# GpSimd takes the low halves of eight weight blocks in the last group of a state-space layer

## The chip, the cores and the metric

The kernel runs on one core of a Trainium2 chip. The metric is the device time of one launch in microseconds (us), and lower is better. The engines of the core work side by side, each through its own instruction queue, and meet only at semaphores: TensorE (PE), VectorE (DVE), ScalarE (ACT), GpSimd (POOL) and SyncE (SP), which here only issues the weight transfers.

## The reference, cut to what matters

A two-layer transformer block (latent attention, a gated recurrence, two MLPs) is followed by a wide layer with three mixers and an MLP, all on 512 tokens, in float32. The third mixer is the state-space one (`ssd_mixer`), and the change lies in it:

```python
xbc = silu(causal_conv(xbc, conv_w, conv_b))
...
cb = einsum('bcign,bcjgn->bcijg', cm, bm)
y_diag = einsum('bcijg,bcijgh,bcjgh,bcjghp->bcighp', cb, lmat, dtc, xs)
...
y_off = einsum('bcign,bcghpn,bcigh->bcighp', cm, h_in, exp(a_cum))
y = y_diag + y_off + xs * d_skip
y = rms_norm_2(y * silu(z), norm_g)
...
gates = sigmoid(mg)
mix = gates[0] * (y_a @ w_br_dsa) + gates[1] * (y_b @ w_br_nsa) + gates[2] * (y_c @ w_br_ssd)
```

`lmat` and `exp(a_cum)` are decays, one 128x128 piece for each of four chunks of 128 tokens and each of 32 heads. The heads come in four groups of eight.

## The kernel before

**Weights.** All weight matrices lie in memory as blocks of 128 x 1024 floats (512 KB). SP streams them into a ring of four slots. A product in float32 is made of three passes of TensorE with rounded operands: high half of the weights by high half of the input (line 366), high by low (367), low by high (368). So each block is split first: `round_block` lets ACT write the high half, `ring_hi`, by one copy of 128x1024 (line 299), and `rest_block` subtracts it from the block and writes the low half, `ring_lo` (line 306). The halves lie in two slots in this stage, so the block n+2 can be rounded only when TensorE is done with block n. The semaphore `blocks_rounded` counts the high halves, and `blocks_split` the low ones, which must come in the order of the blocks whatever engine makes them.

**The state-space layer.** `ssd_pe`, `ssd_act`, `ssd_dve` and `ssd_pool` each write out one engine's part of four groups (`GRPS`) of ten steps (`STEPS`). Group g works on eight heads while the projections of group g+1 run on TensorE between its pieces. In the last group, g = 3, there is nothing left to project, and TensorE computes the eight blocks of the output gate (`ssd_gate`) in steps 0 to 7 in its place; the first two blocks of the next product, `ssd_out`, are split in steps 6 and 7. In a step s of the last group:

- PE: the cumulated decays of head s-1 (lines 2766, 2767); at even steps from 4 on the output of a pair of heads (`output`, lines 2779 and 2783), which waits for DVE's `decay` times `cb` of line 3002 of the step before; then gate block s (24 passes).
- ACT: two exponentials for head s-1, of which the first (line 2868) waits for DVE's differences (line 3012) and the second is line 2870; the copy of gate s out of PSUM (2874); `round_block` of gate block s+2 (299); then the squares of two tiles of y (2887) for the norm at the end, in `squares`. In step 1 the gate's copy and the rounding stand before the exponentials.
- DVE: `decay` times `cb` (3002), four differences (3012), at even steps from 4 on `pair_out` (3039, 3042), then `rest_block` of gate block s+2 (306), then `sums`, which adds ACT's two squares into `ssum` (3031; the first is a copy, 3029). In step 1 the states of the chunks (2979 to 2983) come first, then `rest_block`, then the differences. `sums` leaves out steps 0 and 8.
- POOL: three products in step 0 (3158), and in steps 1 to 8 one product of head s-1's decay with C (3163), `c_dec`, which waits for the first exponential and which PE's `output` needs.

After the last step DVE goes on to `ssd_out_dve` and PE to `ssd_out_pe`. POOL's queue then holds only two transfers, the reload of `h` late in `mix_out` and the store of the result.

```python
        dve.wait_ge(M.sem("blocks_rounded"), ...)
        dve.tensor_tensor(lo, M.ring[:, b % RING, :], hi.bitcast(F32), ALU.subtract).then_inc(M.sem("blocks_split"), 1)
```

Of the kernel before, what the change touches and what calls it, by code (L numbers as in the profile page):

```python
# [17 lines left out]
NT = D // P  # L18
# [15 lines left out]
GRPS, HPG = 4, 8  # L34
# [20 lines left out]
FIRST = {}  # L55
# [26 lines left out]
def splits_before(b):  # L82
    return sum(max(0, min(b, hi) - lo) for lo, hi in SPLITS)
# [199 lines left out]
def split_slot(M, b):  # L283

    if b < FIRST["dsa_in"] or b >= FIRST["ff_up0"]:
        return M.ring_hi[:, b % RING, :], M.ring_lo[:, b % RING, :], RING
    slot = splits_before(b) % 2
    return M.ring2_hi[:, slot, :], M.ring2_lo[:, slot, :], 2
# [13 lines left out]
def rest_block(dve, M, b, i=None, step=0):  # L302

    hi, lo, _ = split_slot(M, b)
    dve.wait_ge(M.sem("blocks_rounded"), (0 if i is None else i * step) + (splits_before(b) + 1))
    dve.tensor_tensor(lo, M.ring[:, b % RING, :], hi.bitcast(F32), ALU.subtract).then_inc(M.sem("blocks_split"), 1)  # L306
# [756 lines left out]
def split_dve(dve, src, hi, lo):  # L1063
    dve.tensor_copy(hi, src)
    dve.drain()
    dve.tensor_tensor(lo, src, hi.bitcast(F32), ALU.subtract)  # L1066
    return dve.drain()
# [1618 lines left out]
def c_dec_of(R, e):  # L2686
    return (R.c_dec + [R.acum, R.dt])[e % 4]
# [259 lines left out]
def ssd_dve(dve, M, R):  # L2947
# [27 lines left out]
    def states(g):  # L2975
        for c in range(N_STATE):
            dve.wait_ge(M.sem("ssd_added"), N_STATE * g + c + 1)
            if c == 0:
                dve.tensor_copy(R.state[1], M.bank(3))
            else:  # L2980
                dve.tensor_tensor(heads(R.state[c + 1]), heads(R.state[c]), by_head(R.chunk_decay, c, g), ALU.mult)
                dve.drain()
                dve.tensor_tensor(R.state[c + 1], R.state[c + 1], M.bank(3 + c), ALU.add)
            dve.drain().then_inc(M.sem("ssd_state"), 1)

    def mix(g, s):
        if s == 0:
            for c in range(QT):
                dve.wait_ge(M.sem("ssd_x_turned"), QT * g + c + 1)
                dve.tensor_tensor(heads(R.x_tok[c]), heads(M.bank(3 + c)), by_head(R.dtc, c, g), ALU.mult)\  # L2990
                   .then_inc(M.sem("ssd_xdt"), 1)
            dve.wait_ge(M.sem("ssd_cb"), g + 1)
            four = lambda x: x.rearrange("p (c i) -> p c i", c=QT)
            dve.tensor_tensor(four(R.cb), four(M.bank(7)), M.t("tri", P).unsqueeze(1).broadcast_to([P, QT, P]),
                              ALU.mult)
            dve.drain()
        if s >= 2:
            e = s - 2
            h = 8 * g + e
            dve.wait_ge(M.sem("ssd_decay"), h + 1)  # L3000
            decay = decay_of(R, g, e)
            dve.tensor_tensor(decay, decay, R.cb, ALU.mult).then_inc(M.sem("ssd_decay_cb"), 1)
        if 1 <= s <= 8:
            e = s - 1
            h = 8 * g + e
            dve.wait_ge(M.sem("ssd_cumulated"), h + 1)
            if h >= 4:
                dve.wait_ge(M.sem("ssd_out_mm"), 2 * (h // 2) - 2)
            for c in range(QT):
                w = slice(c * P, (c + 1) * P)  # L3010

                dve.tensor_scalar(decay_of(R, g, e)[:, w], M.bank(4 + e % 2)[:, w], R.acol[:, c, h:h + 1], 0.0,
                                  ALU.subtract, ALU.min)
            dve.drain().then_inc(M.sem("ssd_seg"), 1)  # L3014
        if s >= 4 and s % 2 == 0:
            pair_out(g, s // 2 - 2)

    def low(ks):
        for k in ks:
            dve.wait_ge(M.sem("tile_rounded"), k + 1 + split_before("ssd_norm"))  # L3020
            dve.scalar_tensor_tensor(out=R.y_lo(k), in0=R.y[:, k, :], scalar=M.c("ssd_norm", k),
                                     in1=R.y_hi(k).bitcast(F32), op0=ALU.mult, op1=ALU.subtract)\
               .then_inc(M.sem("norm_scaled"), 1)

    def sums(s):
        for k in ssd_squares(s):
            dve.wait_ge(M.sem("norm_squared"), k + 1 + M.past("ssd_norm", "squared"))
            if k == 0:
                dve.tensor_copy(M.ssum[:, :], M.sq[:, 0, :])
            else:  # L3030
                dve.tensor_tensor(M.ssum[:, :], M.ssum[:, :], M.sq[:, k % 2, :], ALU.add)
            dve.drain().then_inc(M.sem("norm_summed"), 1)

    def pair_out(g, k):
        pair = 4 * g + k
        dve.wait_ge(M.sem("ssd_gate"), pair + 1)
        dve.wait_ge(M.sem("ssd_out_mm"), 2 * (pair + 1))
        y = R.y[:, pair, :]
        dve.scalar_tensor_tensor(out=y, in0=R.conv[g % 2][k], scalar=M.c("ssd_d", pair),
                                 in1=M.bank(6 if pair % 2 == 0 else 3), op0=ALU.mult, op1=ALU.add)  # L3040
        dve.drain()
        dve.tensor_tensor(y, y, R.gate[g % 2][k], ALU.mult)
        dve.drain().then_inc(M.sem("ssd_y"), 1)
# [48 lines left out]
    for g in range(GRPS):  # L3092
        for s in range(STEPS):
            if s == 1:
                states(g)
            else:
                mix(g, s)
            if s == 9:
                if g + 1 == GRPS:
                    low(range(0, 4))  # L3100
                pair_out(g, 3)
            if g + 1 < GRPS:
                project(g + 1, s)
            elif s < NT:
                rest_block(dve, M, FIRST["ssd_gate"] + s + 2)
            if s == 1:
                mix(g, s)
            if g + 1 == GRPS:
                sums(s)
    ssd_out_dve(dve, M, R, low)  # L3110


def ssd_out_dve(dve, M, R, low):
    dve.drain().then_inc(M.sem("ssd_out_free"), 2)
    rest = lambda b: rest_block(dve, M, FIRST["ssd_out"] + b)
    low(range(4, 12))
    dve.wait_ge(M.sem("norm_root"), 1 + M.past("ssd_norm", "root"))
    dve.reciprocal(M.inv[:, 0:QT], M.root[:, 0:QT]).then_inc(M.sem("norm_inverse"), 1)
    low(range(12, 16))

    def scale(t):
        dve.wait_ge(M.sem("gates_ready"), NT + t + 1)
        dve.tensor_tensor(R.out_gate[t], R.out_gate[t], M.norm_bank("ssd_norm"), ALU.mult)
        dve.drain()

    rest(2)
    dve.wait_ge(M.sem("norm_spread"), 1 + M.past("ssd_norm", "spread"))
    scale(0)
    scale(1)
    for t in range(NT):  # L3130
        if t:
            rest(2 * t + 2)
        dve.wait_ge(M.sem("blocks_used"), FIRST["ssd_out"] + 2 * t + 2)
        m = M.m[:, t, :]
        dve.tensor_tensor(M.ssum[:, :], M.bank(2 * (t % 2) + 1), R.out_gate[t], ALU.mult)
        dve.drain()
        dve.tensor_tensor(m, m, M.ssum[:, :], ALU.add)
        dve.drain().then_inc(M.sem("ssd_out_free"), 1)
        rest(2 * t + 3)
        split_dve(dve, m, M.in_hi[:, t, :], M.in_lo[:, t, :]).then_inc(M.sem("mix_split"), 1)  # L3140
        if t + 2 < NT:
            scale(t + 2)


def ssd_pool(pool, M, R):
    heads = lambda x: x.rearrange("p (h d) -> p h d", d=64)

    def mix(g, s):
        if s == 0:
            if g:  # L3150

                pool.wait_ge(M.sem("ssd_out_mm"), HPG * g)
            for c in range(N_STATE):
                pool.wait_ge(M.sem("ssd_xdt"), QT * g + c + 1)
                if g == 0 and c == 0:
                    pool.wait_ge(M.sem("ssd_to_end"), 1)
                w = R.to_end[:, c, 8 * g:8 * g + 8].unsqueeze(2).broadcast_to([P, 8, 64])
                pool.tensor_tensor(heads(R.xw[c]), heads(R.x_tok[c]), w, ALU.mult).then_inc(M.sem("ssd_xw"), 1)
        if 1 <= s <= 8:
            e = s - 1  # L3160
            pool.wait_ge(M.sem("ssd_exp_c"), 8 * g + e + 1)
            c_dec = c_dec_of(R, e)
            pool.tensor_tensor(c_dec, c_dec, R.conv[g % 2][5], ALU.mult)\
                .then_inc(M.sem("ssd_c_dec"), 1)

    for g in range(GRPS):
        for s in range(STEPS):
            mix(g, s)

# [302 lines left out]
```

## Time and profile before

| | |
|---|---|
| runs | 2938.68, 2944.05, 2943.17 us; median 2943.17 us |
| the profiled execution | 2943.89 us; its span 2942.1 us |
| busy in the span | PE 94%, weight loads 75%, DVE 55%, ACT 39%, POOL 4% |
| the chain that ended last | PE 79%, DVE 11%, ACT 4%, issue 3%, DVE's queue 2% |
| mean granted clock of TensorE | 0.962 |
| steps 1 to 9 of the last group | about 2372 to 2427 us after the span's start |

The span runs from the first to the last instruction; the time of the execution is 1.79 us more. A share of busy time says how much of the span an engine had work in flight. The chain is followed back from the last instruction, at each step to what released it. "Issue" in it is time in which the engine waited for nothing that the profile shows.

### The profile page before, as it was taken

To read this page: it belongs to the slowest core of one execution; us is meant where nothing else is said; L and a number is where in the kernel's file an instruction comes from. 1 tells how busy PE (TensorE), PEld (TensorE's weight loads), DVE (VectorE), ACT (ScalarE), POOL (GpSimd) and SP (SyncE) were. 2 spreads that over 40 slices of the span, in tenths; PEclk is the share of its full clock that TensorE was granted. 3 is DMA by queue.
4 is the path that set the end of the run, shared out by engine and by line. 5 is a ranking of instruction groups with operands and counts; after the bars stand their busy time and mean duration, and the time that the engine had idled before them with its cause. 6 is when DMAs were issued, how large, how long until landed. Compare 5 with 4: busy or idle time off the path is not lost.

```text
span 2942.1 us, 38305 instructions
## 1 busy us (share of the span) xinstructions
PE 2752.9 (94%) x13735; PEld 2213.3 (75%) x13735; DVE 1610.6 (55%) x2960; ACT 1133.8 (39%) x1858; POOL 115.8 (4%) x102
## 2 busy tenths in 40 slices
PE   7999999989999899998998998999899989999998
PEld 5567888877888788887675885667677767778887
DVE  5335726445555672644756347754677765464452
ACT  4344322225554432222437325852255543232221
POOL 0000000000000000000130001000011110000000
PEclk9999999979999999997999989999899999999999
DMA  3112332312111233231120210012222222333231
GB/s 138 42 58 72 107 100 93 100 43 72 57 57 43 72 111 96 93 100 65 57 80 1 87 65 22 1 51 86 72 72 72 65 65 72 115 100 100 93 100 64
DMA packets 59647, 217.76 MB, mean 74 GB/s; under 512 B 6400, under 2 KB 6528, under 8 KB 59392
## 3 DMA queue, kind: packets, MB, share of 16 engines
q1 hardware_dynamic: 57920, 209.76, 22.7%
q0 software_dynamic: 1600, 6.29, 0.6%
q8 instruction: 81, 1.33, 0.2%
q14 instruction: 46, 0.38, 0.0%
HBM read 211.83 MB, written 4.19 MB: 73 GB/s over the span
## 4 chain that ended last, share of the span: by engine, by line
PE 79%; DVE 11%; ACT 4%; issue 3%; DVEq 2%; ACTq 0%; DMA 0%; POOL 0%; SPq 0%
PE ps L366 22%; PE ps L368 22%; PE ps L367 22%; PE ps L447 1%; DVE work L1862 1%; PE ps L500 1%; DVE big L2961 1%; DVE ring_lo L306 1%; DVEq L3014 1%; PE ps L751 1%; PE ps L1331 1%; DVE work L1881 1%; PE ps L455 1%; PE ps L1788 1%; ACT ring_hi L299 1%
## 5 line engine op out<-in xcount | busy, mean ns | idle before, releaser
L366 PE MATMUL ps<-a_hi,ring_hi 128*128 128x512 f32 x1936 | 779.7, 403 | 51.5 <-DVE ring_lo L306 25.4
L368 PE MATMUL ps<-a_hi,ring_lo 128*128 128x512 f32 x1936 | 765.8, 396 | 0.0
L367 PE MATMUL ps<-a_lo,ring_hi 128*128 128x512 f32 x1872 | 739.9, 395 | 0.0
L306 DVE TENSOR_TENSOR ring_lo<-ring,ring_hi 128x1024 fp32r<-128x1024 f32 x360 | 440.3, 1225 | 531.0 <-ACT ring_hi L299 501.7
L299 ACT ACTIVATE ring_hi<-ring 128x1024 fp32r<-128x1024 f32 x378 | 397.6, 1055 | 514.3 <-PE ps L368 512.1
L366 PEld LDWEIGHTS ps<-a_hi,ring_hi 128*128 128x128 f32 x1936 | 371.4, 192 | 134.7 <-issue 21.4
L368 PEld LDWEIGHTS ps<-a_hi,ring_lo 128*128 128x128 f32 x1936 | 370.8, 192 | 80.3
L367 PEld LDWEIGHTS ps<-a_lo,ring_hi 128*128 128x128 f32 x1872 | 359.0, 192 | 74.1 <-issue 1.2
L367 PE MATMUL ps<-hid_lo,ring_hi 128*128 128x512 f32 x960 | 375.5, 391 | 0.0
L366 PE MATMUL ps<-hid_hi,ring_hi 128*128 128x512 f32 x896 | 348.8, 389 | 1.5 <-DVE ring_lo L306 1.5
L368 PE MATMUL ps<-hid_hi,ring_lo 128*128 128x512 f32 x896 | 348.6, 389 | 0.0
L367 PEld LDWEIGHTS ps<-hid_lo,ring_hi 128*128 128x128 f32 x960 | 181.6, 189 | 37.7
L366 PEld LDWEIGHTS ps<-hid_hi,ring_hi 128*128 128x128 f32 x896 | 168.2, 188 | 36.7 <-DVE ring_lo L306 1.9
L368 PEld LDWEIGHTS ps<-hid_hi,ring_lo 128*128 128x128 f32 x896 | 168.2, 188 | 34.8
L1119 ACT ACTIVATE sq<-ps 128x512 f32<-128x512 f32 x96 | 57.5, 599 | 352.7 <-PE ps L368 304.9
L1137 DVE TENSOR_TENSOR ssum<-sq,ps 128x512 f32<-128x512 f32 x96 | 65.8, 685 | 87.8 <-ACT sq L1119 81.6
L1816 ACT ACTIVATE work<-work 128x128 f32<-128x128 f32 (+3 forms) x128 | 70.0, 551 | 11.1 <-DVE work L1866 11.1
L1752 PE MATMUL ps<-big,work 64*128 64x256 f32 (+3 forms) x384 | 64.6, 480 | 10.2 <-DVE work L1866 8.7
L1066 DVE TENSOR_TENSOR hid_lo<-ssum,hid_hi 128x512 f32 (+1 forms) x96 | 66.4, 692 | 12.7 <-issue 1.5
L1139 DVE TENSOR_TENSOR ssum<-ssum 128x512 f32<-128x512 f32 x96 | 66.5, 692 | 7.2
L1752 PEld LDWEIGHTS ps<-big,work 64*128 64x128 f32 x384 | 46.4, 204 | 28.4 <-issue 16.6
L1862 DVE CUSTOM_DVE_ANT_0 work<-ps,work 128x128 f32<-128x128 f32 (+3 forms) x128 | 54.9, 485 | 21.5 <-issue 21.5
(399 smaller groups left out, 3291.2 us busy)
## 6 DMA issues: line engine op xcount, KB each, us to landing
ring<-weights SPq DMA_DIRECT2D x392, 512.0 KB, 3.5
h<-x SPq DMA_DIRECT2D x1, 2048.0 KB, 9.1
residual<-h POOLq DMA_DIRECT2D x2, 1024.0 KB, 4.8
h<-residual POOLq DMA_DIRECT2D x1, 2048.0 KB, 10.9
out<-h POOLq DMA_DIRECT2D x1, 2048.0 KB, 7.8
tab<-tables SPq DMA_DIRECT2D x1, 1648.0 KB, 15.3
big<-positions SPq DMA_DIRECT2D x1, 256.0 KB, 3.5
col<-columns SPq DMA_DIRECT2D x1, 164.5 KB, 4.0
```

Of the source, the lines that this page charges most:

```text
L299: act.activation(hi, M.ring[:, b % RING, :], ACT.Copy).then_inc(M.sem("blocks_rounded"), 1)
L306: dve.tensor_tensor(lo, M.ring[:, b % RING, :], hi.bitcast(F32), ALU.subtract).then_inc(M.sem("blocks_split"), 1)
L366: pe.matmul(out, w_hi, hi, start=start, stop=False)
L367: pe.matmul(out, w_hi, lo, start=False, stop=False)
L368: return pe.matmul(out, w_lo, hi, start=False, stop=stop)
L1066: dve.tensor_tensor(lo, src, hi.bitcast(F32), ALU.subtract)
L1119: act.activation(M.sq[:, u % 2, :], M.bank(u % 4), ACT.Relu).then_inc(free, 1)
L1137: dve.tensor_tensor(M.ssum[:, :], M.sq[:, u % 2, :], M.norm_bank(norm), ALU.mult)
L1139: dve.tensor_tensor(M.ssum[:, :], M.ssum[:, :], M.ssum[:, :], ALU.mult)
L1752: mm = pe.matmul(M.ps[:, at:at + S_LEN[t]], self.staged[rows, u, t * P:(t + 1) * P], self.kinds[kind][0][rows, 0:S_LEN[t]], start=True, st ...
L1816: e = act.activation(s, s, ACT.Exp, bias=V.ntop[:, x, t:t + 1], scale=1.0, accum_out=V.sum[:, x, t:t + 1])
L1862: dve.tensor_tensor_reduce(V.p[x][:, CAUSAL_AT[t]:CAUSAL_AT[t] + S_LEN[t]], M.ps[:, at:at + S_LEN[t]], m[:, CAUSAL_AT[t]:CAUSAL_AT[t] + S_ ...
```

## The change

In the last group, the low halves of gate blocks 2 to 7 and of `ssd_out` blocks 0 and 1 are no longer written by DVE in its steps 0 to 7, but by GpSimd, behind its product of the same step. GpSimd waits once for all earlier low halves, and DVE waits once, ahead of the low half of `ssd_out` block 2, for GpSimd's eight.

```diff
@@ ssd_dve
             if g + 1 < GRPS:
                 project(g + 1, s)
-            elif s < NT:
-                rest_block(dve, M, FIRST["ssd_gate"] + s + 2)
             if s == 1:
                 mix(g, s)
@@ ssd_out_dve
+    dve.wait_ge(M.sem("blocks_split"), splits_before(FIRST["ssd_out"] + 2))
     rest(2)
@@ ssd_pool
     for g in range(GRPS):
         for s in range(STEPS):
             mix(g, s)
+            if g + 1 == GRPS and s < NT:
+                if s == 0:
+                    pool.wait_ge(M.sem("blocks_split"), splits_before(FIRST["ssd_gate"] + 2))
+                rest_block(pool, M, FIRST["ssd_gate"] + s + 2)
```

On DVE, steps 1 and 2 of the last group; `ps` is PSUM, `sq` the squares of ACT:

```order
 L2983 TENSOR_TENSOR work<-work,ps 128x512
-L306 TENSOR_TENSOR ring_lo<-ring,ring_hi 128x1024
 L3012 TENSOR_SCALAR work<-ps,work 128x128 x4
 L3029 COPY ssum<-sq 128x512
```

In step 1 the differences now stand right behind the states, and the copy of the first square behind them.

On DVE, steps 2 to 4, which the later steps repeat:

```order
 L3002 TENSOR_TENSOR work<-work 128x512
 L3012 TENSOR_SCALAR work<-ps,work 128x128 x4
-L306 TENSOR_TENSOR ring_lo<-ring,ring_hi 128x1024
 L3031 TENSOR_TENSOR ssum<-ssum,sq 128x512 x2
 L3002 TENSOR_TENSOR work<-work 128x512
 L3012 TENSOR_SCALAR big<-ps,work 128x128 x4
-L306 TENSOR_TENSOR ring_lo<-ring,ring_hi 128x1024
 L3031 TENSOR_TENSOR ssum<-ssum,sq 128x512 x2
 L3002 TENSOR_TENSOR big<-big,work 128x512
```

The two sums now stand right behind the differences; what they add, `sq`, is written by ACT behind the high half of the block.

On POOL, the last group:

```order
 L3158 TENSOR_TENSOR work<-work 128x512 x3
-L3163 TENSOR_TENSOR work<-work,big 128x512 x8
...
+L306 TENSOR_TENSOR ring_lo<-ring,ring_hi 128x1024
+L3163 TENSOR_TENSOR work<-work,big 128x512
+L306 TENSOR_TENSOR ring_lo<-ring,ring_hi 128x1024
+L3163 TENSOR_TENSOR work<-work,big 128x512
+L306 TENSOR_TENSOR ring_lo<-ring,ring_hi 128x1024
```

The eight products, one behind the other before, now have a low half ahead of each; the first belongs to step 0, and from step 1 on each product is followed by its step's low half.

## Rows read from the trace of the kernel before

**Rows 1.** Busy us by stretch: PE, PEld, DVE, ACT, POOL; then PEclk, DMA share, GB/s.

```profile
2386.50:2401.20 14.70, 13.86 (x82) 11.23 (x82) 10.84 (x19) 7.18 (x12) 2.58 (x2) 1.00 0.23 74
2427.00:2440.00 13.00, 9.51 (x44) 7.80 (x45) 10.81 (x16) 7.55 (x12) 0.00 (x0) 0.52 0.00 1
```

**Rows 2.** The chain that ended last, in step 3: start us, us, what.

```profile
2389.14 0.95 ACT ring_hi L299
...
2390.12 1.22 DVE ring_lo L306
2391.35 0.60 DVEq L3032
```

**Rows 3.** DVE in the last group, in time: start us, us, instruction [idle before].

```profile
2374.25 1.12 DVE L3012 TENSOR_SCALAR work<-ps,work 128x128 f32<-128x128 f32 x4
...
2377.10 0.58 DVE L3029 COPY ssum<-sq 128x512 f32<-128x512 f32 x1 [1.73 <-ACT sq L2887]
...
2378.62 0.69 DVE L3002 TENSOR_TENSOR work<-work 128x512 f32<-128x512 f32 x1
...
2385.75 0.69 DVE L3002 TENSOR_TENSOR work<-work 128x512 f32<-128x512 f32 x1
2386.36 1.12 DVE L3012 TENSOR_SCALAR big<-ps,work 128x128 f32<-128x128 f32 x4
...
2391.26 1.50 DVE L3031 TENSOR_TENSOR ssum<-ssum,sq 128x512 f32<-128x512 f32 x2
2392.88 0.69 DVE L3002 TENSOR_TENSOR big<-big,work 128x512 f32<-128x512 f32 x1
...
2395.62 1.56 DVE L3042 TENSOR_TENSOR big<-big,work 128x512 f32<-128x512 f32 x1
...
2421.86 0.69 DVE L3002 TENSOR_TENSOR big<-big,work 128x512 f32<-128x512 f32 x1
```

**Rows 4.** ACT in steps 1 and 3 of the last group.

```profile
2373.09 1.28 ACT L2868 ACT_TABLE_LOAD   x1
2375.43 0.60 ACT L2868 ACTIVATE work<-ps 128x512 f32<-128x512 f32 x1 [1.06 <-DVEq L3014]
...
2387.54 0.60 ACT L2868 ACTIVATE work<-ps 128x512 f32<-128x512 f32 x1 [3.55 <-DVEq L3014]
...
2389.03 1.06 ACT L299 ACTIVATE ring_hi<-ring 128x1024 fp32r<-128x1024 f32 x1
2389.98 1.15 ACT L2887 ACTIVATE sq<-big 128x512 f32<-128x512 f32 x2
```

**Rows 5.** POOL in time: a low half of an earlier stage, the products of steps 1 and 4.

```profile
1770.73 2.35 POOL L306 TENSOR_TENSOR ring_lo<-ring,ring_hi 128x1024 fp32r<-128x1024 f32 x1 [5.23 <-ACT ring_hi L299]
...
2376.11 1.30 POOL L3163 TENSOR_TENSOR work<-work,big 128x512 f32<-128x512 f32 x1 [16.42 <-ACT work L2868]
...
2395.35 1.29 POOL L3163 TENSOR_TENSOR work<-work,big 128x512 f32<-128x512 f32 x1 [5.84 <-ACT work L2868]
```

**Rows 6.** All low halves of POOL: busy us, mean ns | idle before, releaser.

```profile
L306 POOL TENSOR_TENSOR ring_lo<-ring,ring_hi 128x1024 fp32r<-128x1024 f32 x18 | 43.4, 2412 | 163.3 <-ACT ring_hi L299 163.3
```

**Rows 7.** DVE in time, beside the low half of Rows 5.

```profile
1771.79 1.44 DVE L2543 TENSOR_TENSOR work<-work 128x128 f32<-128x128 f32 x1
```

**Rows 8.** The four instructions of that line: ns min/median/max, first and last start.

```profile
L2543 DVE TENSOR_TENSOR work<-work x4: 293/294/1441, 1762.4 to 1778.1; 128x128 f32<-128x128 f32 x4
```

**Rows 9.** PE in time: decays of step 1, gate block 3, outputs of pairs.

```profile
2371.33 0.40 PE L2766 MATMUL ps<-ssd_sums,ssd_rows 128*128 128x512 f32 x1
...
2378.18 0.39 PE L366 MATMUL ps<-a_hi,ring_hi 128*128 128x512 f32 x1
...
2386.50 0.66 PE L2779 MATMUL ps<-work 128*64 128x128 f32 x8 [2.22 <-DVE work L3002]
...
2401.16 0.66 PE L2779 MATMUL ps<-big,work 128*64 128x128 f32 x8 [0.84 <-DVE big L3002]
...
2427.01 1.12 PE L2779 MATMUL ps<-big,work 128*64 128x128 f32 x8 [9.78 <-DVE big L3002]
```

## The prediction

> **What bounds the kernel now.** The table of the profile says where not to look first: PE is busy 94% of the span and DVE 55%. But the change touches 55 us in which this does not hold, so I read that stage by itself. The busy times by stretch show PE at 13.86 us of 14.70 there, at full granted clock: nearly full, not full [rows 1]. The chain of waits shows who sets the pace: in each step of the last group it goes through DVE's differences, ACT's exponentials, the gate's copy, ACT's high half, DVE's low half and DVE's sums, and back to the differences [rows 2]. PE is not on it; it is the one that waits for DVE's L3002, 2.22 us, 0.84 us and, at the end, 9.78 us [rows 9]. So what is worth anything here is the length of one turn of that chain.
>
> One turn, counted from L3002 of step 3 at 2385.75 (step 4's stands at 2392.88, so a turn is 7.13 us) [rows 3]: the differences end at +1.73 (2386.36 + 1.12); ACT's first exponential starts at +1.79, its high half runs from +3.28 to +4.34, and its two squares start at +4.23 and take 1.15 us, so the first is there at about +4.8 and the second at +5.38 [rows 4]. DVE's low half starts at +4.37 and takes 1.22 us; the first sum ends 0.60 behind it, at +6.20 [rows 2]; the second follows 0.12 later and takes 0.69, and 0.12 later is +7.13. The reader is to see that DVE's low half and ACT's squares run side by side: taking the former away leaves the latter.
>
> **The change part by part.**
>
> *Removed from DVE:* eight low halves. Of 1.22 us each only 0.65 could be won in steps 2 to 7: without them the first sum could start at about +4.86, behind the first square, end at +5.55, the second run to +6.36, and L3002 start at +6.48.
>
> *Added to POOL:* the same eight, at 2.41 us each, the mean of 18 [rows 6]. POOL follows ACT by 0.08 us (exponential 2375.43 + 0.60, product 2376.11) [rows 4, 5], so its low half runs from +4.42 to +6.83. POOL has the time: its product starts at about +2.5 and takes 1.29 us.
>
> *What the two do to each other* decides. In the stage of 1770 us a low half of POOL runs from 1770.73 to 1773.08 [rows 5]. DVE's L2543, which adds two small SBUF tiles, starts at 1771.79 in it and ends at 1773.23: 1.44 us where its median is 0.294 us [rows 7, 8]. It did not go slower in proportion, it ended when POOL had ended. The same in the last group: L3042 starts at 2395.62, beside POOL's product of 2395.35 to 2396.64, and ends at 2397.18 [rows 3, 5], 0.54 us behind POOL's end, about its own 0.69 us less the start. And L3029, a copy between SBUF tiles, takes 0.58 us and ends 0.27 us behind POOL's product, which ends at 2377.41 [rows 3, 5]. So DVE's work whose data all comes from SBUF waits for all of POOL's instruction. The sums of L3031 read two SBUF tiles, but no row of before has one beside POOL: that they wait too is the step I take without a row of their own. I take it because L3042 has the same form and size.
>
> The Trainium skill has this as a rule, in "SBUF — State Buffer", section "SBUF: two separate sides": DVE with two SBUF inputs and a GpSimd instruction that reads SBUF need the same pair of ports, and whichever comes first keeps it for its whole instruction. By that rule the sums wait, and the time is the forecast below; were it not to hold for them, it is the first rival.
>
> *One turn after,* steps 2 to 7: POOL's low half starts at +4.42, ahead of the first sum at +4.86. The sum ends 0.54 behind POOL's end, at +7.37; 0.12 + 0.69 + 0.12 later, at +8.30, is L3002. Six turns are 49.8 us. Before they were 2421.86 - 2378.62 = 43.24 us (two of them hold `pair_out`, which after lies in the same shade of POOL). So +6.56 us.
>
> *Step 1* has another order. DVE's differences no longer wait for the low half: PE's decays are there at about 2372 [rows 9], not 2374.25. ACT can use this only from the end of its table load, 2374.37; the exponential then comes 1.04 us earlier than 2375.43 [rows 4], the first square too, and the copy L3029 is asked for at 2376.06. But POOL's product now runs from 2375.07 to 2376.37, and its low half, 1.29 us behind the exponential instead of ahead of it, stands right behind. The copy ends at 2376.64, POOL holds DVE until 2379.05, the sum L3031 ends at 2379.59, and L3002 of step 2 starts at 2379.71 instead of 2378.62: +1.09 us. Other orders of the three give 2379.7 to 2380.0; I take the first. PE wants gate block 3 at 2378.18 [rows 9] and gets its low half at 2378.8 to 2379.9. This up to 1.7 us is hidden: behind it PE already waited 2.22 us for L3002 of step 3, which now starts 2.25 us later.
>
> *At no cost:* step 0, where POOL's low half (from about 2365) is wanted by PE only at 2372; the waits added on POOL and on DVE, whose counts are reached long before (POOL's eighth low half ends in step 7, two steps ahead of DVE's wait); step 8 and what follows, which have no low half, so all of the shift is passed on. What is queued behind POOL's low halves is its next product, asked for 4 us later. PE needs 2401.16 - 0.84 - 2386.50 = 13.82 us for a pair of heads with two gate blocks [rows 9]; DVE's two turns are then 16.6 us, so PE waits 2.8 us in each pair. If a low half were late for PE it would cost what it is late; the tightest, block 5, is ready at +6.83 of step 3, and PE, which starts its pair's output at +0.75, ends block 4 at about +8 (the output and one block are over half of 13.82).
>
> *Sum:* 6.56 + 1.09 = 7.65 us. The profiled execution's 2943.89 us would become 2951.5. It stands 0.72 us above the median of the runs, so I forecast 2943.17 + 7.65 = 2950.8 us, +0.26%. With a low half of 2.35 us and a stall that costs the sum 0.1 us less it is 6.6 us; if instead the first sum slips in ahead of POOL, POOL runs from +5.55 to +7.96, the second sum ends at +8.50 and the turn is 8.62 us, 9.6 us in all. So 2949.8 to 2952.8 if the mechanism holds.
>
> **The rivals.**
>
> *The sums do not wait (not slower).* Then the turn is 6.48 us, six are 38.9, which is 4.4 less than 43.24, and step 1 gives 1.04: -5.4 us, 2937.8 us. PE gives part of it back, since its 13.82 us for a pair are more than 12.96; I bound this case at -3.5 to -5.4 us, 2937.8 to 2939.7. For it: no row shows a sum beside POOL. Against it: L2543, L3042 and L3029. The point from which it decides: the sums end no later than before only if POOL holds them for less than about 1.2 us of its 2.41.
>
> *PE's granted clock falls.* PE would be busy 13.82 of 16.6 us, with gaps of 2.8 us. Behind the idle 9.78 us the granted clock is 0.52, the lower of its two levels [rows 1]; beside the gaps of 2.22 and 0.84 us it stays at 1.00. If it fell once in the middle, a gate block of 24 passes at 0.23 us would take up to some 5 us more, and the gaps absorb 2.8: 2 to 7 us on top, 2953 to 2958 us.
>
> *The extra is hidden.* The last group's end would have to be set by something else. PE's 9.78 us wait for L3002 of step 9 speaks against it, and so does the chain, which has no other member there. If half the turn's extra went unseen, the time would be about 2947.
>
> **How the numbers follow.** Forecast 0.80, the sums free 0.09, the clock 0.06, hidden in part 0.05. A measurement of this kernel can tell 0.2%, 5.9 us, from no change. The forecast's own range lies above it, by 0.7 us at the low end, so I leave 0.03 of it in "same". Slower: 0.77 + 0.06 = 0.83. Free sums straddle 0.2% from the other side, with most of their range within it: faster 0.04, same 0.05. So same is 0.03 + 0.05 + 0.05 = 0.13. The range reaches from halfway into the hidden case, with the scatter of the runs (5.4 us) in mind, to the middle of the clock's: 2945.5 to 2956. What lies in its lower part would be scatter; that part holds none of the free sums.
>
> **What would show it.** Right: on DVE the first L3031 of a step takes about 2.5 us in place of 0.69; eight POOL L306 of 2.4 us in the last group, each 0.08 us behind ACT's; L3002 every 8.3 us; PE's waits for L3002 near 2.8 us, and the last near 11. Wrong: L3031 at 0.69 us beside a running POOL L306 (first rival); passes of 0.43 us in a gate block (second); L3002 of step 2 at 2377.6 instead of 2379.7 (my reading of step 1); or a POOL L306 that itself is stretched by DVE, for which I have no price of its own in this stage.

## The result, and the profile after

| | before | changed |
|---|---|---|
| median of 16 runs | 2941.13 us (2936.57 to 2946.00) | 2948.55 us (2945.51 to 2953.40) |
| ratio | | 1.0026, 95% interval 1.0019 to 1.0033 |
| profiled execution, its span | 2943.89, 2942.1 us | 2945.70, 2943.9 us |

The changed kernel is 7.4 us slower by the medians, 0.25%. The forecast was +7.65 us and 2950.8 us. All 16 runs of before have a median 2 us below that of the three runs that the forecast started from, so the absolute time is 2.3 us lower than forecast and the difference 0.2 us. One of all the runs used here was slow, 3051.86 us at a granted clock of 0.878 (of the kernel "half a low half" below), and it is in no ratio.

The two profiled spans differ by 1.8 us only, since the profiled execution of before was 2.8 us above its median and that of the changed kernel 2.9 us below. So the spans can't be compared as a whole. A mark in DVE's program ahead of anything that the change touches shows why: L2994, the last product of step 0, starts at 2351.34 us, where it started at 2358.21 in the profile of before. The execution was 6.87 us ahead when it came to the stage, in code that is the same in both, which is within the scatter of the runs. I therefore measure the stage inside each profile, from the start of that L2994 to the start of DVE's first low half behind the group (of `ssd_out` block 2): 2449.28 - 2358.21 = 91.07 us before, 2449.80 - 2351.34 = 98.46 us after. That is +7.39 us, the whole of the loss. Each stage here is measured in one profile. Its last 23 us vary by up to 0.6 us from kernel to kernel with TensorE's clock (last section), so smaller differences are read at L3002, where that plays no part.

DVE in the changed kernel, in time (start us, us, instruction, idle before), which answers to [rows 3]:

```profile
2351.34 0.68 DVE L2994 TENSOR_TENSOR work<-ps,tab 128x512 f32<-128x512 f32 x1
...
2358.34 2.90 DVE L2981 TENSOR_TENSOR work<-work 128x512 f32<-128x512 f32 x1 [0.17 <-PE ps L2753]
...
2369.19 0.58 DVE L3029 COPY ssum<-sq 128x512 f32<-128x512 f32 x1 [2.93 <-ACT sq L2887]
2369.89 2.68 DVE L3031 TENSOR_TENSOR ssum<-ssum,sq 128x512 f32<-128x512 f32 x1
2372.69 0.69 DVE L3002 TENSOR_TENSOR work<-work 128x512 f32<-128x512 f32 x1
...
2377.59 3.26 DVE L3031 TENSOR_TENSOR ssum<-ssum,sq 128x512 f32<-128x512 f32 x2 [3.17 <-ACT sq L2887]
2380.96 0.69 DVE L3002 TENSOR_TENSOR work<-work 128x512 f32<-128x512 f32 x1
...
2385.86 3.30 DVE L3031 TENSOR_TENSOR ssum<-ssum,sq 128x512 f32<-128x512 f32 x2 [3.16 <-ACT sq L2887]
2389.27 0.69 DVE L3002 TENSOR_TENSOR big<-big,work 128x512 f32<-128x512 f32 x1
...
2397.94 0.69 DVE L3002 TENSOR_TENSOR big<-big,work 128x512 f32<-128x512 f32 x1 [0.47 <-issue]
...
2422.78 0.69 DVE L3002 TENSOR_TENSOR big<-big,work 128x512 f32<-128x512 f32 x1
...
2427.18 0.69 DVE L3002 TENSOR_TENSOR big<-big,work 128x512 f32<-128x512 f32 x1
...
2449.80 1.23 DVE L306 TENSOR_TENSOR ring_lo<-ring,ring_hi 128x1024 fp32r<-128x1024 f32 x1 [4.14 <-ACT ring_hi L299]
```

The two sums of a step took 1.50 us and take 3.3. DVE has one instruction less in each turn, is idle longer ahead of the sums (3.17 us for ACT's square where it was 2.65 for the high half), and yet a turn, from L3002 to L3002, is 8.27 and 8.31 us in steps 2 and 3, where it was 7.13.

POOL and the chain of waits of the changed kernel show what the sums wait for:

```profile
2349.77 3.05 POOL L3158 TENSOR_TENSOR work<-work 128x512 f32<-128x512 f32 x3 [12.35 <-DVE work L2990]
2358.31 2.39 POOL L306 TENSOR_TENSOR ring_lo<-ring,ring_hi 128x1024 fp32r<-128x1024 f32 x1 [5.49 <-ACT ring_hi L299]
...
2368.20 1.29 POOL L3163 TENSOR_TENSOR work<-work,big 128x512 f32<-128x512 f32 x1 [7.50 <-ACT work L2868]
2369.44 2.58 POOL L306 TENSOR_TENSOR ring_lo<-ring,ring_hi 128x1024 fp32r<-128x1024 f32 x1
...
2383.43 1.27 POOL L3163 TENSOR_TENSOR work<-work,big 128x512 f32<-128x512 f32 x1 [3.95 <-ACT work L2868]
2385.39 2.40 POOL L306 TENSOR_TENSOR ring_lo<-ring,ring_hi 128x1024 fp32r<-128x1024 f32 x1 [0.69 <-ACT ring_hi L299]
```

```profile
2384.36 0.95 ACT ring_hi L299
2385.31 0.53 ACT sq L2887
2385.83 0.02 issue
2385.86 2.48 DVE ssum L3031
2388.34 0.03 DVEq L3032
2388.37 0.09 issue
2388.46 0.69 DVE ssum L3031
```

The first sum is asked for at 2385.86, when POOL's low half has run for 0.47 us. POOL ends at 2387.79, and the sum at 2388.34, 0.55 us later; it took 2.48 us. The second sum, which meets nothing, takes 0.69. In the chain, the sum stands where the low half of DVE stood in [rows 2]. No semaphore joins the sum and POOL's low half, so here two engines meet outside the semaphores, and the profile shows it as a longer instruction, not as idle time.

The same happens once in step 1, which the prediction did not foresee: L2981, which reads two SBUF tiles, is asked for at 2358.34, when the low half of step 0 has just begun, and takes 2.90 us in place of 0.69, to 0.54 us behind POOL's end. It costs nothing, for the differences behind it wait for PE anyway, until 2365.13.

PE in the changed kernel, which answers to [rows 9]:

```profile
2372.16 0.47 PE L366 MATMUL ps<-a_hi,ring_hi 128*128 128x512 f32 x1 [0.69 <-POOL ring_lo L306]
...
2381.71 1.12 PE L2779 MATMUL ps<-work 128*64 128x128 f32 x8 [3.35 <-DVE work L3002]
...
2398.68 0.66 PE L2779 MATMUL ps<-big,work 128*64 128x128 f32 x8 [1.63 <-DVE big L3002]
...
2415.29 0.82 PE L2779 MATMUL ps<-work 128*64 128x128 f32 x8 [2.76 <-DVE work L3002]
...
2427.93 1.12 PE L2779 MATMUL ps<-big,work 128*64 128x128 f32 x8 [9.68 <-DVE big L3002]
```

PE waits longer for DVE in the middle of the group, and once, for 0.69 us, for POOL's low half of gate block 3.

### The profile page after: what moved, and what is told of

It reads as the page before. It is cut to its first block, busy times and chain, and to the rows that moved or that the text cites. A ratio compares the mean times of both kernels' runs of the same rounds, so it can differ in the third digit from the quotient of the medians.

```text
span 2943.9 us, 38307 instructions
## 1 busy us (share of the span) xinstructions
PE 2748.8 (93%) x13735; PEld 2210.2 (75%) x13735; DVE 1616.9 (55%) x2952; ACT 1134.3 (39%) x1858; POOL 135.0 (5%) x110
## 3 DMA queue, kind: packets, MB, share of 16 engines
HBM read 211.83 MB, written 4.19 MB: 73 GB/s over the span
## 4 chain that ended last, share of the span: by engine, by line
PE 79%; DVE 11%; ACT 4%; issue 3%; DVEq 2%; ACTq 0%; DMA 0%; POOL 0%; SPq 0%
PE ps L366 22%; PE ps L367 21%; PE ps L368 21%; PE ps L447 1%; DVE work L1862 1%; PE ps L500 1%; DVE big L2961 1%; DVEq L3014 1%; PE ps L751 1%; PE ps L1331 1%; DVE work L1881 1%; DVE ring_lo L306 1%; PE ps L455 1%; PE ps L1788 1%; DVE ssum L3031 1%
## 5 line engine op out<-in xcount | busy, mean ns | idle before, releaser
L306 DVE TENSOR_TENSOR ring_lo<-ring,ring_hi 128x1024 fp32r<-128x1024 f32 x352 | 430.6, 1225 | 509.3 <-ACT ring_hi L299 480.1
L306 POOL TENSOR_TENSOR ring_lo<-ring,ring_hi 128x1024 fp32r<-128x1024 f32 x26 | 62.7, 2411 | 171.5 <-ACT ring_hi L299 171.5
```

## The experiments

Eight kernels were run, each beside the kernel before. The ratio is to that kernel, "in us" is the ratio less 1 times its median, 2941.7 us, and the stage is measured in each profile as above (before 91.07 us, changed 98.46 us). An interval is 1.7 to 2.9 promille wide, 5 to 9 us, so the finer readings rest on the stage.

| kernel | ratio, 95% interval | in us | stage, against 91.07 |
|---|---|---|---|
| sums in PSUM | 0.9987 (0.9978 to 0.9995) | -3.8 | 87.85, -3.2 |
| later sums, low halves on DVE | 0.9976 (0.9965 to 0.9987) | -7.1 | 84.17, -6.9 |
| later sums, low halves on GpSimd | 0.9967 (0.9955 to 0.9980) | -9.7 | 82.37, -8.7 |
| step 1 back on DVE | 1.0021 (1.0012 to 1.0030) | +6.2 | 97.99, +6.9 |
| GpSimd fills beside | 1.0006 (0.9997 to 1.0016) | +1.8 | 91.53, +0.5 |
| GpSimd reads beside | 1.0050 (1.0036 to 1.0065) | +14.7 | 105.32, +14.3 |
| half a low half | 1.0001 (0.9993 to 1.0010) | +0.3 | 91.17, +0.1 |
| later sums in PSUM, on GpSimd | 0.9970 (0.9959 to 0.9981) | -8.8 | 82.39, -8.7 |

**Sums in PSUM.** The changed kernel, with the running sum in a free PSUM bank, so that a sum has one input from SBUF instead of two:

```diff
-            if k == 0:
-                dve.tensor_copy(M.ssum[:, :], M.sq[:, 0, :])
-            else:
-                dve.tensor_tensor(M.ssum[:, :], M.ssum[:, :], M.sq[:, k % 2, :], ALU.add)
+            total = M.ssum[:, :] if k == 15 else M.bank(2)
+            if k == 0:
+                dve.tensor_copy(total, M.sq[:, 0, :])
+            else:
+                dve.tensor_tensor(total, M.bank(2), M.sq[:, k % 2, :], ALU.add)
```

> The changed kernel, but the running sum of the squares lies in a PSUM bank until its last addition, so that a sum reads one SBUF tile instead of two. Stall theory (DVE waits for GpSimd only with data all from SBUF): the sums run free beside the low half, the next stall is that of L3002, which ends 0.54 us behind GpSimd; a turn is then about 6.7 us instead of 8.3, and the time is about 3 us below the kernel before (10 us below the changed one). Rival (GpSimd's hold stops any DVE instruction that reads SBUF): no change against the changed kernel, 7 to 8 us above before.

DVE, and POOL's low half beside it:

```profile
2388.12 1.52 DVE L3032 TENSOR_TENSOR ps<-ps,sq 128x512 f32<-128x512 f32 x2 [3.16 <-ACT sq L2887]
2389.76 0.85 DVE L3002 TENSOR_TENSOR big<-big,work 128x512 f32<-128x512 f32 x1
```

```profile
2387.65 2.41 POOL L306 TENSOR_TENSOR ring_lo<-ring,ring_hi 128x1024 fp32r<-128x1024 f32 x1 [0.66 <-ACT ring_hi L299]
```

The same two sums, asked for 0.47 us behind the start of the same low half, take 1.52 us and don't wait. L3002, with two inputs from SBUF, asks 0.30 us ahead of POOL's end, at 2390.06, and ends 0.55 us behind it. So what waited was not the sum as such but the second input from SBUF. The edit also moves the sum's output into PSUM, but L2994 above shows that this is not what frees it: it has one input from SBUF, writes to SBUF, and takes 0.68 us while POOL's three products of 2349.77 run. The changed kernel with this one edit is 10.6 us faster by the medians (7.4 above before, now 3.2 below; 3.8 by the ratio), and faster than the kernel before. The rival, that POOL stops every DVE instruction that reads SBUF, is out.

**Later sums, on either engine.** DVE adds the squares of step s-1 in step s, ahead of what it waits for in this step; those of step 7 follow L3002 of step 9. It is the same edit in the kernel before (with the low half kept) and in the changed one:

```diff
+            if g + 1 == GRPS and 2 <= s <= 7:
+                sums(s - 1)
...
-            if g + 1 == GRPS:
+            if g + 1 == GRPS and s == 9:
                 sums(s)
```

> The kernel before, but DVE adds the squares of step s-1 in step s, ahead of its low half, so that no sum stands between the low half and the next differences. If the length of the turn of DVE and ACT sets the pace, the stage is bound by PE's 13.8 us for a pair of heads, and DVE's last L3002 comes some 7 us earlier: 5 to 9 us below the kernel before. If PE or ACT sets the pace already: within 1 us of it.

> The changed kernel with the same later sums. Stall theory: the two sums and the next L3002 are asked for before GpSimd's low half begins or while PE is the bound, so GpSimd's low half costs little or nothing: 7 to 10 us below the kernel before, like the late sums with the low half on DVE or up to 2 us better. Rival (GpSimd's low half costs by being late for PE, not by the stall of the sums): 5 us or more above the late sums with the low half on DVE.

Both came as expected. In the first of the two PE has no wait left in steps 2 to 8, and its last for L3002 is 5.81 us, where it was 9.78:

```profile
2370.00:2384.00 14.00, 14.00 (x83) 11.38 (x82) 11.93 (x22) 8.66 (x16) 3.68 (x4) 1.00 0.24 77
2384.00:2398.00 14.00, 14.00 (x83) 11.38 (x82) 12.58 (x20) 7.82 (x13) 3.48 (x3) 1.00 0.28 87
...
```

These are the busy times by stretch: PE is busy for all of 28 us. So the turn of DVE and ACT was the bound in the kernel before, and the order of DVE's work set its length.

With the low half on POOL, DVE is stalled still, for example here:

```profile
2402.22 4.19 DVE L3031 TENSOR_TENSOR ssum<-ssum,sq 128x512 f32<-128x512 f32 x2 [0.50 <-ACT sq L2887]
2406.54 0.69 DVE L3002 TENSOR_TENSOR big<-big,work 128x512 f32<-128x512 f32 x1
```

The sums take 4.19 us, more than in the changed kernel, since the first meets POOL's low half (2401.76 to 2404.18) and the second its next product (2404.13 to 2405.87), and yet the kernel is 9.7 us faster than before. A stall costs only where the stalled instruction is on the path. The stage is 1.8 us shorter than with the low half on DVE: 1.32 of it at L3002 of step 9, and 0.48 behind it. The intervals of the two ratios overlap, so that GpSimd helps here rests on one profile of each and not on the times.

**Step 1 back on DVE.** The changed kernel, with seven low halves on POOL and that of step 1 on DVE, as before:

```diff
+            elif s == 1:
+                dve.wait_ge(M.sem("blocks_split"), splits_before(FIRST["ssd_gate"] + 3))
+                rest_block(dve, M, FIRST["ssd_gate"] + s + 2)
```

> The changed kernel with the low half of step 1 back on DVE, the other seven on GpSimd. By the prediction's sum step 1 is worth 1.09 us of 7.65, so this is 6.6 us above the kernel before. If all eight low halves cost the same, it would be 0.9 us less than the changed kernel too; the two are told apart by L3002 of step 2, which by the prediction comes as in the kernel before, 6.9 to 7.0 us behind the start of step 1's rounding on ACT, where it was 7.5 in the changed kernel.

L3002 of step 2 starts at 2373.10, which is 20.47 us behind L2994 (2352.63); before it was 20.41, changed 21.35. So step 1 costs 0.88 us at L3002 of step 2 (1.09 in the sum). Behind the start of ACT's rounding of step 1 it stands 6.66 us (2366.44), against 7.53 in the changed kernel and 6.60 before; I had written 6.9 to 7.0 for the first, misread from the rows. At the end of the stage the difference is 0.47 us only, 98.46 against 97.99, since the last 23 us took 22.62 us there and 22.98 here (last section). The times can't tell it: 1.0021 and 1.0026 lie within each other's interval.

**GpSimd beside DVE's own low half.** Twice the kernel before, with nothing moved; POOL gets something useless to do in steps 0 to 7, woken by the same high half. Once it fills an unused table twice, which reads nothing, once it subtracts two tiles of 128x1024, which reads two:

```diff
+            if g + 1 == GRPS and s < NT:
+                b = FIRST["ssd_gate"] + s + 2
+                if s == 0:
+                    pool.wait_ge(M.sem("blocks_split"), splits_before(b))
+                pool.wait_ge(M.sem("blocks_rounded"), splits_before(b) + 1)
+                pool.memset(M.t("causal", BLK * P), 0.0)
+                pool.drain()
+                pool.memset(M.t("causal", BLK * P), 0.0)
+                pool.drain()
```

The second kernel has in place of the two fills:

```diff
+                pool.tensor_tensor(M.t("causal", BLK * P), M.a2_lo[:, 0:2, :].rearrange("p a b -> p (a b)").bitcast(F32), M.a2_lo[:, 2:4, :].rearrange("p a b -> p (a b)").bitcast(F32), ALU.subtract)
+                pool.drain()
```

> The kernel before, with DVE still doing its low halves, and in steps 0 to 7 of the last group GpSimd also fills 1024 columns of an unused table twice, woken by the same high half; it reads no SBUF. If only a GpSimd instruction that reads holds DVE's SBUF pairs: L306 and L3031 keep 1.22 and 0.69 us, and the time stays within 1 us of before. If any GpSimd instruction holds them: L306 or the first sum is stretched to the end of a fill, 1 us or more in each of six turns, 6 us or more in all.

> The kernel before, with DVE still doing its low halves, and in steps 0 to 7 of the last group GpSimd also subtracts two 128x1024 tiles that nobody needs, woken by the same high half: the hold alone, with nothing taken off DVE and nothing that PE waits for. Stall theory: DVE's L306 goes first (0.05 us earlier), GpSimd starts behind it and holds DVE's sums and L3002 for its 2.41 us: 2.1 to 2.3 us in each of six turns and about 2 in step 1, 13 to 16 us above before. Rival (the changed kernel is slower since the low half itself is late): no change from before.

DVE with the fills, and POOL's fills of the same turn:

```profile
2382.40 1.23 DVE L306 TENSOR_TENSOR ring_lo<-ring,ring_hi 128x1024 fp32r<-128x1024 f32 x1 [2.65 <-ACT ring_hi L299]
2383.54 1.50 DVE L3031 TENSOR_TENSOR ssum<-ssum,sq 128x512 f32<-128x512 f32 x2
```

```profile
2382.43 0.96 POOL L3174 MEMSET tab<- 128x1024 f32 x1 [0.64 <-ACT ring_hi L299]
2383.50 0.95 POOL L3176 MEMSET tab<- 128x1024 f32 x1
```

All of DVE's instructions there have two inputs from SBUF, all overlap a fill, and none is longer. The stage is 0.5 us longer all the same, and L3002 of step 9 0.92: 0.89 of that comes from the copy of step 1, which the fill did hold up (last section). By the ratio it is 1.8 us, more than the 1 us expected, with an interval that includes zero. And with the subtraction:

```profile
2380.58 1.23 DVE L306 TENSOR_TENSOR ring_lo<-ring,ring_hi 128x1024 fp32r<-128x1024 f32 x1 [2.65 <-ACT ring_hi L299]
2381.72 3.64 DVE L3031 TENSOR_TENSOR ssum<-ssum,sq 128x512 f32<-128x512 f32 x2
2385.48 0.69 DVE L3002 TENSOR_TENSOR work<-work 128x512 f32<-128x512 f32 x1
```

```profile
2380.62 3.38 POOL L3174 TENSOR_TENSOR tab<-a_lo 128x1024 f32<-128x1024 f32 x1 [0.65 <-ACT ring_hi L299]
```

POOL asks 0.04 us behind DVE, waits for the low half, runs, and the sum waits for it in turn: 14.3 us in all, as expected. (In steps 4 and 6 POOL came first, unlike what I expected, and DVE's low half itself took 3.12 and 3.46 us; these turns are 9.44 and 9.43 us, the others 9.28 to 9.34.) Nobody needs what POOL computes here, and PE never waits for a low half in the stage, so the lateness of one has no part in it. This is the stall by itself.

**Half a low half.** The changed kernel, in which POOL writes only columns 0 to 511 of each of the eight low halves; the rest keeps the values of an earlier block, so that part of the gate and of the output product is left out.

```diff
-                rest_block(pool, M, FIRST["ssd_gate"] + s + 2)
+                half_rest_block(pool, M, FIRST["ssd_gate"] + s + 2)
```

> The changed kernel, but GpSimd writes only the first 512 of the 1024 columns of each of the eight low halves, so the rest of them holds old values. The hold is then 1.29 us instead of 2.41, which is close to the point from which it decides by the prediction (about 1.2 us): a turn of 7.2 us and L3002 of step 2 as before, so within 1 us of the kernel before. If the hold were no stall but a slowdown by a share, or if the loss had a fixed part per instruction of GpSimd, it would stay 3 to 5 us above.

```profile
2376.88 2.19 DVE L3039 TENSOR_TENSOR ssum<-ssum,sq 128x512 f32<-128x512 f32 x2 [3.17 <-ACT sq L2895]
```

```profile
2376.41 1.30 POOL L306 TENSOR_TENSOR ring_lo<-ring,ring_hi 128x512 fp32r<-128x512 f32 x1 [0.66 <-ACT ring_hi L299]
```

(L3039 is L3031 here, by eight lines added above it.) Six turns are 2415.49 - 2371.99 = 43.50 us, before 43.24, and the stage is 0.10 us longer. With a hold of 1.29 us the move neither costs nor brings anything, which fits the point from which it decides, put at about 1.2 us. A fixed cost for each of GpSimd's instructions is out, since as many of them cost next to nothing here. So is a slowdown by a share: the two sums less the second (0.69) and the gap (0.12) leave 1.38 us for the first, which ends at 2378.26, again 0.55 us behind POOL's end at 2377.71.

**Both remedies.** The later sums and the sums in PSUM together, low halves on POOL.

> The changed kernel with the later sums and the sums in PSUM together. If PE's work is the bound with the later sums alone, this adds nothing: 9 to 11 us below the kernel before, as the later sums with the low half on GpSimd. If stalls of the sums still stood in the way there, it is 1 to 3 us below that one.

It adds nothing to the later sums alone, 82.39 us against 82.37: once PE is the bound, the stalls of the sums cost nothing. (By the ratio it is 8.8 us below before, a little short of the 9 to 11 expected.)

## Why the prediction was right

- *What bounds the stage.* The turn of DVE and ACT, not PE. Shown by the later sums, which shorten the turn and take 6.9 us out of the stage.
- *The sums wait for all of POOL's instruction.* This was the step without a row of its own, and it decided the sign. The rows of after show it (2.48 us in place of 0.69, ending 0.55 us behind POOL; the forecast assumed 0.54), and the sums in PSUM, the fills and the subtraction show what it takes: two inputs from SBUF on DVE, and a POOL instruction that reads. The rule of the Trainium skill ("SBUF — State Buffer", section "SBUF: two separate sides") says both halves, two inputs and a GpSimd instruction that reads, and the runs agree with it. So the first rival is out, and its price of -5.4 us with it.
- *Six turns, 49.8 us.* They took 2422.78 - 2372.69 = 50.09 us. Single turns are 8.24 to 8.31 us against 8.30, except one of 8.67 (2389.27 to 2397.94). The kernel before has a longer one at the same place, 7.54 us; I took it out of the turns after by the shade of POOL. That was wrong by 0.3 us: DVE's idle 0.47 us in it, most of which the chain calls "issue", is there in both.
- *Step 1, +1.09 us.* L3002 of step 2 came 0.94 us later, measured from L2994. The order was as taken: product, copy, then POOL's low half, which was itself 2.58 us long beside the copy (2.35 to 2.41 in the other steps), and a sum of 2.68 us.
- *At no cost.* PE was late for gate block 3 by 0.85 us, counted from L2994 (2372.16 and 2378.18), against 0.6 to 1.7, and the wait for L3002 of step 3 hid it. Step 0 cost nothing, though its low half did hold up DVE (L2981, above): the prediction had not looked for this, and DVE happened to have the time.
- *The rest is passed on.* L3002 of step 9 is 7.79 us later (75.84 against 68.05 us behind L2994), and the end of the stage 7.39. The sum had 7.65 at both: 0.3 too little in the turns, 0.15 too much in step 1, and 0.40 us won back at the end, which it didn't have.
- *PE's waits.* I expected 2.8 us each and 11 at the end; they are 3.35, 1.63, 2.76 and 9.68. The first is longer since L3002 of step 3 comes 2.08 us later, and gate block 3 only 0.85. For 1.63 and 9.68 the clock is the reason. In the output of 2381.71 PE's first eight products took 1.12 us, in that of 2398.68 0.66 us: at the end of the wait of 3.35 us the granted clock had fallen to the lower level, 0.51 from 2381.7 to 2385.0. That output took 3.19 us up to the gate block behind it (2384.90), the one of 2398.68 1.68 us, and the 1.5 us are missing in the next wait. The output of 2415.29, behind the wait of 2.76 us, lost 1.2 us the same way out of the wait of 9.68. So the second rival did occur, for the length of an output, and cost nothing, since PE had the time. I had put its price at 2 to 7 us by taking that a whole gate block would be hit.
- *The range* held the time. Its lower part, below 2949.8 us, was meant for scatter, and the median lies in it, since the three runs that I started from were 2 us high. That the difference came out within 0.3 us is in part luck: 0.3 too little in the turns, 0.15 too much in step 1 and 0.4 at the end offset each other.

## What to carry to other kernels

Before DVE's work is moved to GpSimd, list what DVE will do while GpSimd does it. In this kernel each DVE instruction with two inputs from SBUF waited to the end of a GpSimd instruction that reads SBUF. So the move pays only where DVE has other work or waits anyway for as long as GpSimd takes, here 2.41 us where DVE took 1.22. An idle GpSimd is no free place beside a chain that comes back to DVE within that time. And where a turn between two engines is the bound, look first at what DVE does between its answer and the next question: putting the sums off by one step brought more (6.9 us) than either place for the low half, and made the move harmless.

## What the runs showed of the hardware

- A fill by GpSimd, which reads nothing, does not hold up DVE's instructions with two inputs from SBUF. But it holds up a DVE copy from SBUF to SBUF: in the run with the fills, the copy of step 1 took 1.48 us (0.58 before), to 0.28 us behind the end of POOL's fill. It was asked for while POOL's product ran (until 2375.91), and the fill then came first; in the changed kernel the copy came ahead of POOL's low half at the same place. What decides that order is not shown.

```profile
2375.61 1.48 DVE L3029 COPY ssum<-sq 128x512 f32<-128x512 f32 x1 [1.73 <-ACT sq L2887]
```

```profile
2375.86 0.95 POOL L3174 MEMSET tab<- 128x1024 f32 x1
```

- The end of the stage, from L3002 of step 9 to the first low half of DVE, took 23.02 us before and 22.62 changed, with the same instructions. What differs is PE's clock. In the kernel before its passes go over to the upper level (0.39 us for 0.63) at 2439.43, 5.69 us behind the first pass of `ssd_out` at 2433.74; changed, at 2439.50, 4.83 us behind that pass at 2434.67. A pass follows the last in 0.43 us at the lower level and 0.23 at the upper, so 0.86 us less at the lower is worth about 0.4 us (an estimate). Other profiles bear it out. The seventeenth pass starts 6.46 us behind the first in the kernel before, 5.99 in the changed one, and 6.20, 6.36, 5.99, 5.87 and 6.40 with the sums in PSUM, step 1 on DVE, the fills, the reads and half a low half; the end of the stage took 23.02, 22.62, 22.84, 22.98, 22.56, 22.42 and 23.03 us, which is 16.55 to 16.64 us more each time. Why the clock rises at another point in each is open.
- DVE's idle 0.47 us in the third turn, from step 4 to step 5, is in both kernels and in most of the variants, but ahead of different instructions: before, with the fills and with the reads ahead of the low half of step 4, in the changed kernel ahead of L3002 of step 5. What it is stays open.
